# A down projection turned from 96 weight units into 24 rounds of seven products, in a one-core encoder block

## The chip, the cores and the metric
One core of a Trainium2 chip runs the whole block as one program. The metric is the device time of an execution in microseconds.

## The reference, cut to what matters
The block is one layer on x of 512 tokens x 2048 channels, float32: a mixer (attention and a gated recurrence), then a convolutional gated MLP.

```python
h = rmsnorm(x, norm_ffn_pre)
g = causal_dwconv(h @ w_gate, conv_ffn_w, conv_ffn_b)      # w_gate, w_up: 2048 x 6144
y = (gelu(g) * (h @ w_up)) @ w_down                        # w_down: 6144 x 2048
x = x + rmsnorm(y, norm_ffn_post)
```
The change is in the last two lines. The mixer ahead of them keeps its work.

## The kernel before, in words
Every float32 operand of a large product is split into a high part (a ScalarE copy into the matmul's reduced float32 form) and a low part (VectorE: operand minus high part). A product of two 128x128 by 128x256 tiles is three matmuls: high by high, high by low, low by high (`product`, L1816 to L1818). Weights come in units of 128 x 1024 numbers, 512 KB, each partition's 4 KB contiguous in memory. SyncE's queue (SP) issues the weight loads, GpSimd's queue (POOL) issues adding DMAs and stores and reloads of intermediates. Each engine follows its own program in written order and waits on semaphores; `split_done` counts finished low halves of weights and `unit_used` units that TensorE has finished.

**Gate and up projections.** The 48 hidden tiles (128 channels each) are computed 6 plainly and 42 in the seven-product loop (`for i in range(NS)`, NS = 42). A round multiplies a 2 x 2 arrangement of weight blocks by a 2 x 2 arrangement of activation blocks with seven block products instead of eight. Each of the seven is 8 tile products of three matmuls. The rows of the weight arrangement are the gate (A11, A12) and the up (A21, A22) columns of a tile, the four weight sums are S1 = A21 + A22, S2 = S1 + A11, S3 = A21 + A11 and S4 = S2 + A12 (signs are in the operands). S1 and S3 come by a plain load of one block (SP) and an adding DMA of the other onto it (POOL, `add_to_s1`, `add_to_s3`); S2 and S4 are VectorE additions (`form_s2`, `form_s4`). raw_s1 has two buffers, all the others one. SP issues per round i, in this order: S1 (after A22 of the round before), A11 (after the low half of product 0 of round i-1), S3 (after that of product 3), A12 (product 4), A22 (product 6). The high half of product k waits until TensorE has finished product k-3, since the split weights have three places (`w_slot`). The product's regions of the accumulators are taken out by VectorE (and one by ScalarE), become the gate tile, and with convolution and GELU the hidden tile, which POOL stores (`store_h`).

**Down projection.** Four groups of 512 output channels, each 24 units of 256 hidden channels. In a unit, two hidden tiles (reloaded by `load_h`) are the stationary side, as 128 hidden x 128 tokens, and the unit's weights move: 4 banks x 2 halves x 2 tiles x 3 matmuls. y stands with tokens in the partitions. **End.** Sums of squares per token along the row, root and reciprocal, scaling, transposes of y to channels in partitions (`lift`), and VectorE's addition onto x1 (L1807), from where SP stores it.

Of the kernel before, what the change touches and what calls it, by code (L numbers as in the profile page):

```python
# [29 lines left out]
P = 128  # L30
# [31 lines left out]
N_OUT, N_FF, N_FAST, N_HID = U_OUT - U_MIX, U_FF - U_MIX, U_FAST - U_MIX, U_HID - U_MIX  # L62
MORE_MIX = (32, 32)
# [33 lines left out]
H_STEP = 2 * S + 6 * LINE // 4  # L97
# [36 lines left out]
def block_kernel(nc, xT, par_d, weights, gate_w, out):  # L134
    negc_d = nc.dram_tensor("negc", [2 * NP, S], F32, kind="Internal").ap()
    h_d = nc.dram_tensor("h_spill", [FT, P, S], F32, kind="Internal").ap()

    with ExitStack() as ctx:
# [6 lines left out]
        def sem(name):  # L145
# [7 lines left out]
        eps_y = sb("eps_y", [QT])  # L153
# [11 lines left out]

        level = w_all[:, LINE // 4:4 * UW + LINE // 4].rearrange("p (b x) -> p b x", b=2)
        wd_hi, wd_lo = [[level[:, :, S * c:S * c + S] for c in (2 + part, part)] for part in range(2)]
# [5 lines left out]
        DOWN_BANKS = (banks[0:4], banks[4:8])  # L173

        region_a = ExitStack()
        act_hi = sb_in(region_a, "act_hi", [KT, S], F32R)
        act_lo = sb_in(region_a, "act_lo", [KT, S], F32R)
        region_a.close()  # L180
        sb("act_hi_first", [KT // 2, S])
        y_a = sb("y_a", [2, D])
        sb("act_lo_first", [KT // 2, S])
        y_b = sb("y_b", [2, D])
# [61 lines left out]

        ffn = ExitStack()
# [4 lines left out]
        sb_in(ffn, "rest_of_x1_6_7", [UW - HS])  # L252
# [11 lines left out]
        hid = ExitStack()  # L264
        h_t = sb_in(hid, "h_t", [FT, S])
        sb_in(hid, "last_hidden_tile", [5, S])
        y_sq = sb_in(hid, "y_sq", [GROUPS, QT])
        y_p = sb_in(hid, "y_p", [2, QT])
        y_r = sb_in(hid, "y_r", [QT])
        y_s = sb_in(hid, "y_s", [QT])  # L270
        hid.close()
        fin = ExitStack()
        x1_b = sb_in(fin, "x1_b", [KT, S])
        fin.close()

# [3 lines left out]
            wf_landed wf_hi_done wf_split f_done f_low_done f_taken f_ready f_lifted f_negabs f_exp f_logs f_back negc_ready negc_stored negc_spread negc_copied  # L279
# [15 lines left out]
         wf_landed, wf_hi_done, wf_split, f_done, f_low_done, f_taken, f_ready, f_lifted, f_negabs, f_exp, f_logs,  # L295
         f_back, negc_ready, negc_stored, negc_spread, negc_copied,
# [7 lines left out]
         gate_taken, tap_done, conv_done, gelu_done, h_done, h_hi_done, h_split, x1_gained, t_formed,  # L304
         t_hi_done, t_split,
         a11_landed, a12_landed, a22_landed, s3_half, s3_landed, s2_done, s4_done,
         p1_copied, pu_done, pw_done, c22_done, c11_taken, c12_done, c21_done, last_done,
         wd_taken, wdsq_done, y_summed, y_std_done, y_r_done, y_scaled_a, y_scaled_d, diag_done, spread_done,
         eps_y_done, x1_back_landed, lifted, taken,
# [6 lines left out]
        h_stored = [sem(f"h_stored{s}") for s in range(2)]  # L316
        h_landed = [sem(f"h_landed{s}") for s in range(PER_GROUP // 2)]
        s1_half = [sem(f"s1_half{s}") for s in range(2)]
        s1_landed = [sem(f"s1_landed{s}") for s in range(2)]

# [9 lines left out]
        def two_tiles(t, ku):  # L330
            return t[:, bass.ds(ku * 2, 2), :].rearrange("p a s -> p (a s)")

# [9 lines left out]
        def y_tile(i):  # L342
            return y_a[:, i] if i < 2 else y_b[:, i - 2]

        def h_half(t, s):

            c = 4 * S * s + HS - 7 * LINE // 4
            t = flat(t)[:, c:c + 2 * H_STEP].rearrange("p (b x) -> p b x", b=2)[:, :, 0:2 * S]  # L350
            return t.rearrange("p b (a n) -> p b a n", n=S)[:, :, :, 0:HS]

        def h_tokens(t, s, kt, i):

            c = 4 * S * s + HS - 7 * LINE // 4 + H_STEP * kt + S * (i // 2) + P * (i % 2)
            return flat(t)[:, c:c + P]

        def halves(t):
            return t.rearrange("p (b a n) -> p b a n", b=2, n=HS)

# [13 lines left out]
        w3_hi, w3_lo = k_tiles(w_3[:, 0]), k_tiles(w_3[:, 1])  # L374

# [7 lines left out]
        def _(sp):  # L383
# [69 lines left out]
            for i in range(NS):  # L453

                u, q = U_FF + 4 * (PLAIN + i), N_FAST + 7 * (i - 1)
# [8 lines left out]
                sp.dma_start(raw[:, 0], weights[u]).then_inc(a11_landed, 16)  # L464
# [4 lines left out]
                sp.dma_start(raw_s3[:], weights[u + 2]).then_inc(s3_half, 16)  # L469
                sp.wait_ge(split_done, q + 5 if i else N_FAST)  # L470
                sp.dma_start(raw[:, 1], weights[u + 1]).then_inc(a12_landed, 16)
# [4 lines left out]
                sp.dma_start(raw_a22[:], weights[u + 3]).then_inc(a22_landed, 16)  # L476
            sp.wait_ge(split_done, N_HID - 6)
            sp.dma_start(raw[:, 0], weights[U_DOWN]).then_inc(raw_landed[0], 16)
            sp.wait_ge(split_done, N_HID - 2)
            sp.dma_start(raw[:, 1], weights[U_DOWN + 1]).then_inc(raw_landed[1], 16)  # L480
            with sp.Fori(1, GROUPS * PER_GROUP // 2) as t:
                for s in range(2):

                    sp.wait_ge(split_done, t * 2 + (N_HID + s - 1))
                    sp.dma_start(raw[:, s], weights[bass.ds(t * 2 + (U_DOWN + s), 1)].rearrange(
                        "a p n -> p (a n)")).then_inc(raw_landed[s], 16)

            for k in range(KT):
                sp.wait_ge(taken, k + 1)
                sp.dma_start(out[:, k], x1_b[:, k]).then_inc(stored, 16)  # L490
# [4 lines left out]
        def _(pool):  # L495
# [26 lines left out]
            with pool.Fori(1, NP) as p:  # L522
                pool.wait_ge(gw_split, p)
                pool.dma_start(gw[:], gate_w[bass.ds(p, 1)].rearrange("a p m n -> p (a m) n")).then_inc(gw_landed, 16)
                pool.wait_ge(s_taken, p * 6)
                pool.dma_start(negc[:], negc_d[bass.ds(p * 2, 2)].partition_broadcast(P)).then_inc(negc_landed, 16)
# [7 lines left out]
            def store_h(j):  # L534
                pool.wait_ge(h_done, j + 1)
                pool.dma_start(h_d[j], h_out[:, j % 2]).then_inc(h_stored[j % 2], 16)

            def add_to_s1(i):
                pool.wait_ge(s1_half[i % 2], i // 2 * 16 + 16)
                pool.dma_start(raw_s1[:, i % 2], weights[U_FF + 4 * (PLAIN + i) + 3], accum_op=ALU.add).then_inc(  # L540
                    s1_landed[i % 2], 16)

            def add_to_s3(i):
                pool.wait_ge(s3_half, 16 * i + 16)
                pool.dma_start(raw_s3[:], weights[U_FF + 4 * (PLAIN + i)], accum_op=ALU.add).then_inc(s3_landed, 16)

            for j in range(PLAIN - 2):
                store_h(j)
            add_to_s1(0)
            add_to_s3(0)  # L550
            store_h(PLAIN - 2)
            add_to_s1(1)
            for i in range(NS):
                store_h(PLAIN - 1 + i)
                if i + 1 < NS:
                    add_to_s3(i + 1)
                if i + 2 < NS:
                    add_to_s1(i + 2)

            def load_h(n):  # L560
                for e in range(2):
                    pool.wait_ge(h_stored[e], 16 * n + 16)
                half = PER_GROUP // 2
                at_least(pool, h_hi_done, n - half + 1)
                pool.dma_start(h_t[:, 2 * n:2 * n + 2], h_d[2 * n:2 * n + 2].rearrange("a p s -> p a s")).then_inc(
                    h_landed[n % half], 16)

            pool.wait_ge(unit_used, N_HID - 3)
            for n in range(4):
                load_h(n)  # L570
            for n in range(4, PER_GROUP):
                pool.wait_ge(unit_used, N_HID + n - 4)
                load_h(n)
                if n == 8:
                    store_h(FT - 1)

            pool.wait_ge(x1_stored, 16 * KT)
            for q in range(4):
# [1784 lines left out]
```

## Time and profile before

| | |
|---|---|
| median of 3 runs | 2187.09 us (2187.03 to 2187.22) |
| span of the profiled execution | 2186.0 us |
| TensorE / VectorE / ScalarE / GpSimd busy | 2171.7 / 1529.4 / 1002.2 / 141.7 us |
| gate/up loop | from 828 to 1638 us |
| down projection | from 1638 to 2168 us |

The span is the profiled execution's own time; the median of the runs stands 1.1 us above it. Busy matmul time overlaps itself, since matmuls are pipelined (a matmul is shown with 276 ns, and the next starts 0.113 us after it), so the distance between matmuls is read from counts in a window, and not from their mean duration.

### The profile page before, as it was taken

To read this page: it belongs to the slowest core of one execution; us is meant where nothing else is said; L and a number is where in the kernel's file an instruction comes from. 1 tells how busy PE (TensorE), PEld (TensorE's weight loads), DVE (VectorE), ACT (ScalarE), POOL (GpSimd) and SP (SyncE) were. 2 spreads that over 40 slices of the span, in tenths; PEclk is the share of its full clock that TensorE was granted. 3 is DMA by queue.
4 is the path that set the end of the run, shared out by engine and by line. 5 is a ranking of instruction groups with operands and counts; after the bars stand their busy time and mean duration, and the time that the engine had idled before them with its cause. 6 is when DMAs were issued, how large, how long until landed. Compare 5 with 4: busy or idle time off the path is not lost.

```text
span 2186.0 us, 45684 instructions
## 1 busy us (share of the span) xinstructions
PE 2171.7 (99%) x18942; PEld 2154.4 (99%) x18942; DVE 1529.4 (70%) x2030; ACT 1002.2 (46%) x1278; POOL 141.7 (6%) x210
## 2 busy tenths in 40 slices
PE   9999999999999999999999999999999999999998
PEld 8999999999999999999999999999999999999998
DVE  7776777778755977888888888888885444444445
ACT  6555555447322554444444444444443343343433
POOL 0000000000100001111111111111111100000000
PEclk9999999999999999999999999999999999999999
DMA  5222222222432437777777777777767632222343
GB/s 175 91 99 94 85 92 95 89 96 87 150 112 97 163 116 203 209 214 210 209 203 206 209 206 207 209 214 204 204 178 219 192 113 97 96 96 96 99 170 116
DMA packets 100850, 329.01 MB, mean 151 GB/s; under 512 B 13024, under 2 KB 20832, under 8 KB 100208
## 3 DMA queue, kind: packets, MB, share of 16 engines
q1 hardware_dynamic: 75456, 240.06, 31.9%
q0 software_dynamic: 22672, 82.36, 17.5%
q10 hardware_dynamic: 2592, 4.72, 0.6%
q8 instruction: 98, 1.61, 0.3%
q14 instruction: 32, 0.26, 0.0%
HBM read 306.09 MB, written 21.00 MB: 150 GB/s over the span
## 4 chain that ended last, share of the span: by engine, by line
PE 97%; DVE 2%; ACT 1%; issue 0%; POOL 0%; DVEq 0%; ACTq 0%; POOLq 0%
PE bank L1816 31%; PE bank L1818 31%; PE bank L1817 31%; PE bank L1901 1%; PE bank L1914 1%; PE bank L1926 0%; DVE x_b L1807 0%; PE bank L1925 0%; PE bank L1986 0%; ACT w_all L589 0%; DVE w_all L1058 0%; PE bank L1872 0%; PE bank L2004 0%; PE bank L2003 0%; PE bank L1932 0%
## 5 line engine op out<-in xcount | busy, mean ns | idle before, releaser
L1816 PE MATMUL bank<-act_hi,w_all 128*128 128x256 f32 x2832 | 786.3, 278 | 1.7 <-DVE act_lo L1530 0.9
L1818 PE MATMUL bank<-act_hi,w_all 128*128 128x256 f32 x2832 | 782.2, 276 | 0.0
L1817 PE MATMUL bank<-act_lo,w_all 128*128 128x256 f32 x2832 | 782.1, 276 | 0.0
L1816 PEld LDWEIGHTS bank<-act_hi,w_all 128*128 128x128 f32 x2832 | 531.6, 188 | 5.4 <-issue 2.5
L1817 PEld LDWEIGHTS bank<-act_lo,w_all 128*128 128x128 f32 x2832 | 531.7, 188 | 0.4
L1818 PEld LDWEIGHTS bank<-act_hi,w_all 128*128 128x128 f32 x2832 | 531.6, 188 | 0.0
L1816 PE MATMUL bank<-w_all,act_hi 128*128 128x256 f32 x1536 | 424.0, 276 | 0.1
L1818 PE MATMUL bank<-w_all,act_lo 128*128 128x256 f32 x1536 | 423.9, 276 | 0.0
L1817 PE MATMUL bank<-w_all,act_hi 128*128 128x256 f32 x1536 | 423.9, 276 | 0.0
L1068 DVE TENSOR_TENSOR w_all<-raw,w_all 128x1024 fp32r<-128x1024 f32 x95 | 116.4, 1226 | 279.5 <-ACT w_all L595 279.5
L1816 PEld LDWEIGHTS bank<-w_all,act_hi 128*128 128x128 f32 x1536 | 288.3, 188 | 0.3 <-issue 0.3
L1817 PEld LDWEIGHTS bank<-w_all,act_hi 128*128 128x128 f32 x1536 | 288.3, 188 | 0.0
L1818 PEld LDWEIGHTS bank<-w_all,act_lo 128*128 128x128 f32 x1536 | 288.3, 188 | 0.0
L1058 DVE TENSOR_TENSOR w_all<-raw,w_all 128x1024 fp32r<-128x1024 f32 x134 | 164.1, 1224 | 135.8 <-ACT w_all L589 133.9
L1816 PE MATMUL bank<-tsum,w_all 128*128 128x256 f32 x896 | 247.3, 276 | 0.0
L1817 PE MATMUL bank<-tsum,w_all 128*128 128x256 f32 x896 | 247.3, 276 | 0.0
L1818 PE MATMUL bank<-tsum,w_all 128*128 128x256 f32 x896 | 247.3, 276 | 0.0
L595 ACT ACTIVATE w_all<-raw 128x1024 fp32r<-128x1024 f32 x95 | 100.9, 1062 | 288.3 <-PE bank L1818 283.4
L589 ACT ACTIVATE w_all<-raw 128x1024 fp32r<-128x1024 f32 x133 | 140.5, 1057 | 168.0 <-PE bank L1818 165.8
L963 ACT ACTIVATE w_all<-raw_s 128x1024 fp32r<-128x1024 f32 x112 | 119.0, 1062 | 154.0 <-PE bank L1818 149.6
L1677 DVE TENSOR_TENSOR w_all<-raw_s,w_all 128x1024 fp32r<-128x1024 f32 x112 | 137.2, 1225 | 44.8 <-ACT w_all L963 43.4
L1816 PEld LDWEIGHTS bank<-tsum,w_all 128*128 128x128 f32 x896 | 168.2, 188 | 0.0
(297 smaller groups left out, 3707.0 us busy)
## 6 DMA issues: line engine op xcount, KB each, us to landing
raw<-weights SPq DMA_DIRECT2D x310, 512.0 KB, 3.3
raw_s<-weights SPq DMA_DIRECT2D x84, 512.0 KB, 5.0
raw_s<-weights POOLq DMA_DIRECT2D x84, 512.0 KB, 5.7
raw_a<-weights SPq DMA_DIRECT2D x42, 512.0 KB, 5.5
h_spill<-h_out POOLq DMA_DIRECT2D x48, 256.0 KB, 3.4
h_t<-h_spill POOLq DMA_DIRECT2D x24, 512.0 KB, 4.1
x<-xT POOLq DMA_DIRECT2D x16, 256.0 KB, 3.9
out<-x ACTq DMA_DIRECT2D x16, 256.0 KB, 2.3
```

Source lines behind the costliest of these rows:

```text
L589: act.activation(w_hi[s], k_tiles(raw[:, s]), ACT.Copy).then_inc(hi_done, 1)
L595: act.activation(wd_hi[s], out_cols(raw[:, s]), ACT.Copy).then_inc(hi_done, 1)
L963: act.activation(w_slot(q)[0], k_tiles(RAW_OF[n](i)), ACT.Copy).then_inc(hi_done, 1)
L1058: dve.tensor_tensor(w_lo[s], k_tiles(raw[:, s]), word(w_hi[s]), ALU.subtract).then_inc(split_done, 1)
L1068: dve.tensor_tensor(wd_lo[s], out_cols(raw[:, s]), word(wd_hi[s]), ALU.subtract).then_inc(split_done, 1)
L1677: dve.tensor_tensor(lo, k_tiles(RAW_OF[n](i)), word(hi), ALU.subtract).then_inc(split_done, 1)
L1816: pe.matmul(dst, ah, bh, start=start, stop=False, skip_group_check=goes_on)
L1817: pe.matmul(dst, ah, bl, start=False, stop=False, skip_group_check=goes_on)
L1818: return pe.matmul(dst, al, bh, start=False, stop=stop, skip_group_check=goes_on)
L1901: last[e] = pe.matmul(dst, q, k, start=t == 0, stop=t == 2)
L1914: last = pe.transpose(dst, sm[:, c:c + P], ident[:])
```

## The change
The down projection goes through the same loop: NF = NS + 24 rounds. A round computes two tiles of 128 output channels over a chunk of 16 hidden tiles (8 pairs); three chunks (CH = 3) x eight pairs of output tiles (PAIRS_OUT = 8). The seven moving operands of a chunk (quadrants and sums of the hidden tiles) are formed when the hidden tiles are: per pair of tiles VectorE makes the differences in place (`t_of_pair`, `t3_of_pair`), and POOL stores seven parts of 128 KB (`store_pair`, `store_t3`). For each chunk POOL loads them back, 1 MB each (`load_t`), into the places of the operands that the chunk before no longer needs; ScalarE and VectorE split them in place (`t_n_hi`, `t_n_lo`), between the weight halves, as `T_AFTER` says. The weights keep their layout in memory, so a block of 128 x 1024 for a pair of output tiles is now 1024 pieces of 128 numbers (512 B), for plain and for adding DMAs. y has channels in partitions now; its partial sums of the first two chunks go to memory (the second by an adding store), come back as `Y_TILES` and are completed in the third chunk. The ending has no transposes: squares are summed by matmuls, the reciprocal roots are spread over the partitions by two matmuls, 16 tiles are scaled by VectorE, and the additions onto x1 are 4 on VectorE and 12 on GpSimd. A few semaphores of the mixer are merged, and one POOL loop there is written out.

```diff
+CH = 3
+CK = UK
+PAIRS_OUT = KT // 2
+ND = CH * PAIRS_OUT
+NF = NS + ND
+T_AFTER = {1: 5, 2: 6, 3: 7, 4: 8, 5: 9, 6: 10}
...
+        OPERANDS = ((P00, T0, T1, T2, P10, P11, T3), (P01, P00, T0, T1, T2, P10, P11), (T3, P01, P00, T0, T1, T2, P10),
+                    (P11, T3, P01, P00, T0, T1, P10))
+        def t_free_after(c, n):
+            last = N_FAST + 7 * (NS - 1 + PAIRS_OUT * c)
+            if n == 0:
+                return last - 7 if c else N_FAST
+            return last + 7 if c == CH - 1 and n == 6 else last + n
+        def down_weights(i, r, kh):
+            c, o = (i - NS) // PAIRS_OUT, (i - NS) % PAIRS_OUT
+            u, n = U_DOWN + o // 2 * PER_GROUP + CK * c, o % 2 * 2 * P + r * P
+            return weights[u:u + CK].rearrange("u p (t n) -> t p u n", t=2)[kh][:, :, n:n + P]
...
 SP:
-            for i in range(NS):
+            for i in range(NF):
-                sp.dma_start(raw_s1[:, i % 2], weights[u + 2]).then_inc(s1_half[i % 2], 16)
+                if i < NS:
+                    sp.dma_start(raw_s1[:, i % 2], weights[u + 2]).then_inc(s1_half[i % 2], 16)
+                else:
+                    sp.dma_start(in_k(raw_s1[:, i % 2]), down_weights(i, 1, 0)).then_inc(s1_half[i % 2], 16)
...
 POOL:
+            def load_t(c, n):
+                pool.wait_ge(unit_used, t_free_after(c, n))
+                m = CK * (c + 1)
+                for stored_t, each in ((to_stored, 16), (te_stored, 16), (tq_stored, 32), (t3_stored, 16)):
+                    pool.wait_ge(stored_t, each * m)
+                pool.dma_start(operand(NS + PAIRS_OUT * c, n)[3], t_d[c, T_PLACE[n]].rearrange("p (k n) -> p k n", n=HS)).then_inc(t_landed[n], 16)
...
+            for i in range(NF):
+                if i <= NS:
+                    store_after(PLAIN - 1 + i)
+                elif i == NS + 1:
+                    store_t3(HT - 1)
+                c, o = (i + 1 - NS) // PAIRS_OUT, (i + 1 - NS) % PAIRS_OUT
+                if i >= NS - 2 and c + 1 < CH and o == PAIRS_OUT - 1:
+                    load_t(c + 1, 0)
+                if i > NS and i - 1 < NS + 2 * PAIRS_OUT:
+                    store_y(i - 1)
+                at_boundary = i >= NS - 1 and c < CH and o == 0
+                if at_boundary:
+                    load_t(c, 1)
+                if i + 1 < NF:
                     add_to_s3(i + 1)
+                if i + 2 < NF:
                     add_to_s1(i + 2)
+                if at_boundary:
+                    for n in range(2, 6):
+                        load_t(c, n)
+                    if c == CH - 1:
+                        load_y(0)
+                        load_y(1)
+                    load_t(c, 6)
+                if i == NS + 2 * PAIRS_OUT:
+                    for t in range(2, KT):
+                        load_y(t)
...
 ACT (and DVE alike, with the low halves):
+            def t_n_hi(c, n):
+                act.wait_ge(t_landed[n], 16 * c + 16)
+                hi, _, _, summed = operand(NS + PAIRS_OUT * c, n)
+                act.activation(hi, summed, ACT.Copy).then_inc(th_done, 1)
+            def t_n_after(i, n, convert):
+                k = 7 * (i - (NS - 1)) + n
+                for c in range(CH):
+                    if k == 7 * PAIRS_OUT * c - 2:
+                        convert(c, 0)
+                    for m in range(1, 7):
+                        if k == 7 * PAIRS_OUT * c + T_AFTER[m]:
+                            convert(c, m)
+            def hi(i, n):
+                if i < NF:
+                    product_hi(i, n)
+                    t_n_after(i, n, t_n_hi)
...
 DVE, the first region of b in the third chunk, and the end:
+                dve.wait_ge(y_back[o if o < 2 else 0], 32 if o < 2 else 32 + 16 * (KT - 4))
+                chain(dve.tensor_tensor(ya[:, HS:], ya[:, HS:], p1[:], ALU.add))
+                chain(dve.tensor_tensor(in_two(yb), in_two(yb), p1[:].unsqueeze(1).broadcast_to([P, 2, HS]), ALU.subtract))
+                dve.wait_ge(unit_used, N_FAST + 7 * i + 2)
+                dve.tensor_tensor(ya[:, HS:], ya[:, HS:], b, ALU.add).then_inc(pu_done, 1)
+            for t in range(KT):
+                y = Y_TILES[t]
+                dve.scalar_tensor_tensor(out=y, in0=y, scalar=col("g_ffn_post", t), in1=banks[1][:], op0=ALU.mult,
+                                         op1=ALU.mult).then_inc(z_done, 1)
+                if t in ADD_BY_DVE:
+                    dve.wait_ge(z_done, t + 1)
+                    dve.tensor_tensor(x1_place(t), x1_place(t), in_two(y), ALU.add).then_inc(taken_d, 1)
...
 TensorE:
-            for i in range(NS):
+            for i in range(NF):
+                if i >= NS:
+                    pe.wait_ge(tn_split, (i - NS) // PAIRS_OUT * 7 + n + 1)
...
-            for g in range(GROUPS):
-                n, out_banks = g * PER_GROUP, DOWN_BANKS[g % 2]
...
```

## Rows read from the trace of the kernel before

**Rows 1.** The page: span, busy time, and the chain that ended last.
```profile
span 2186.0 us, 45684 instructions
PE 2171.7 (99%) x18942; PEld 2154.4 (99%) x18942; DVE 1529.4 (70%) x2030; ACT 1002.2 (46%) x1278; POOL 141.7 (6%) x210
PE 97%; DVE 2%; ACT 1%; issue 0%; POOL 0%; DVEq 0%; ACTq 0%; POOLq 0%
```
**Rows 2.** Windows: us, busy (count) of PE, PEld, DVE, ACT, POOL, clock, DMA, GB/s.
```profile
1000.00:1200.00 200.00, 200.00 (x1767) 200.00 (x1767) 164.76 (x200) 93.77 (x107) 25.22 (x33) 1.00 0.75 206
...
1900.00:2100.00 200.00, 200.00 (x1767) 200.00 (x1766) 90.94 (x82) 80.17 (x90) 1.65 (x3) 1.00 0.33 111
```
**Rows 3.** Groups by line, down projection: first of its three matmul lines.
```profile
L1816 PE MATMUL bank<-w_all,act_hi 128*128 128x256 f32 x1536 | 424.0, 276 | 0.1
```
**Rows 4.** Timelines of TensorE, VectorE, ScalarE in one round: start, us, instruction, idle before.
```profile
998.35 0.28 PE L1816 MATMUL bank<-act_hi,w_all 128*128 128x256 f32 x1
...
1010.58 1.23 DVE L1677 TENSOR_TENSOR w_all<-raw_a,w_all 128x1024 fp32r<-128x1024 f32 x1 [0.27 <-ACT w_all L963]
...
1013.62 1.22 DVE L1677 TENSOR_TENSOR w<-raw,w 128x1024 fp32r<-128x1024 f32 x1
...
1020.37 1.06 ACT L963 ACTIVATE w<-raw_s 128x1024 fp32r<-128x1024 f32 x1 [0.95 <-PE bank L1818]
```
**Rows 5.** Groups by line and shape, VectorE and ScalarE, 840 to 1640 us.
```profile
L1687 DVE TENSOR_TENSOR raw_s<-raw_s,raw 128x1024 f32<-128x1024 f32 x42 | 51.1, 1217 | 4.0 <-DMA raw_s<-weights 4.0
...
L1734 DVE TENSOR_TENSOR up<-pv,bank 128x256 f32<-128x256 f32 x42 | 17.7, 421 | 1.4
...
L963 ACT ACTIVATE w_all<-raw_s 128x1024 fp32r<-128x1024 f32 x112 | 119.0, 1062 | 154.0 <-PE bank L1818 149.6 <-DVE raw_s L1687 4.4
```
**Rows 6.** Timeline of SP's queue: two loads of 1024 pieces, then one round.
```profile
16.02 3.15 SPq L417 DMA_DIRECT2D ev<-weights  x2
...
1003.67 0.33 SPq L469 DMA_DIRECT2D raw_s<-weights  x1
...
1011.83 0.33 SPq L476 DMA_DIRECT2D raw_a<-weights  x1
1012.20 0.50 SPq L460 DMA_DIRECT2D raw_s<-weights  x1
```
**Rows 7.** Timeline of POOL in the same round; group of the hidden tiles' reload.
```profile
1007.58 0.58 POOL L536 DMA_DIRECT2D h_spill<-h_out  x1 [7.08 <-DVE h_out L1704]
1008.14 0.91 POOL L545 DMA_DIRECT2D raw_s<-weights  x1
1018.95 0.86 POOL L540 DMA_DIRECT2D raw_s<-weights  x1 [9.90 <-DMA raw_s<-weights]
...
L565 POOL DMA_DIRECT2D h_t<-h_spill x24 | 17.1, 712 | 96.5 <-PE bank L1818 91.0 <-issue 5.4
```
**Rows 8.** DMA in windows 5.5 to 7, 10 to 15, 1000 to 1100 us.
```profile
q1 hardware_dynamic: 465, 0.24, 63.0%
...
DMA packets 985, 1.94 MB, mean 388 GB/s; under 512 B 77, under 2 KB 656, under 8 KB 985
...
q0 software_dynamic: 1980, 7.08, 37.8%
q1 hardware_dynamic: 3609, 13.14, 37.1%
```
**Rows 9.** DMA issues: transfer, count, size, median us to landing.
```profile
raw_s<-weights POOLq DMA_DIRECT2D x84, 512.0 KB, 5.7
...
x_b<-out POOLq DMA_DIRECT2D x4, 1024.0 KB, 5.7
```
**Rows 10.** The window after TensorE's last work.
```profile
2181.00:2184.00 3.00, 0.00 (x0) 0.00 (x0) 0.86 (x2) 0.00 (x0) 0.00 (x0) 0.50 1.03 381
```
**Rows 11.** Timelines of ScalarE and VectorE at the end.
```profile
2168.49 0.60 ACT L1004 ACTIVATE sq<-bank 128x512 f32<-128x512 f32 x1
...
2171.24 10.62 DVE L1807 SCALAR_TENSOR_TENSOR x_b<-bank,par,x_b 128x512 f32<-128x512 f32 x16
```

More of the change, by code:

```diff
@@ L245, in block_kernel @@
         spare.close()
+        plain = ExitStack()
+        tsum_f32 = sb_in(plain, "tsum_f32", [4, 2, UK, HS])
+        plain.close()
         ffn = ExitStack()
@@ new lines, in store_y @@
+            def store_y(i):
+                n = i - NS
+                for done in (c11_taken, c12_done, c22_done, c21_done):
+                    pool.wait_ge(done, i + 1)
+                if n == PAIRS_OUT:
+                    for e in range(2):
+                        pool.wait_ge(y_stored[e], 16 * PAIRS_OUT)
+                for half in range(2):
+                    t = n % PAIRS_OUT * 2 + half
+                    if n < PAIRS_OUT:
+                        pool.dma_start(y_d[t], Y_STAGE[n % 2][half]).then_inc(y_stored[n % 2], 16)
+                    else:
+                        pool.dma_start(y_d[t], Y_STAGE[n % 2][half], accum_op=ALU.add).then_inc(y_stored[n % 2], 16)
@@ L583, in _ @@
+                if i == NS + 2 * PAIRS_OUT:
+                    for t in range(2, KT):
+                        load_y(t)
+            adds = [t for t in range(KT) if t not in ADD_BY_DVE]
+            pool.wait_ge(x1_back, 16 * KT)
+            for t in adds:
+                pool.wait_ge(z_done, t + 1)
+                pool.tensor_tensor(x1_place(t), x1_place(t), in_two(Y_TILES[t]), ALU.add).then_inc(taken_p, 1)
         @block.scalar
@@ new lines, in _ @@
+                hi(i + 1, 0)
+                hi(i + 1, 1)
+            act.activation(cols[:, 0, 0:1], eps[:, 0:1], ACT.Sqrt)
+            ya, yb = Y_TILES[KT - 2], Y_TILES[KT - 1]
+            act.wait_ge(yacc_added, KT - 2)
+            for done, src, dst in ((c22_done, yb[:, HS:], pu[:]), (c11_taken, ya[:, 0:HS], sq[:, 1, 0:HS]),
+                                   (c12_done, ya[:, HS:], sq[:, 1, HS:S]), (c21_done, yb[:, 0:HS], pv[:])):
+                act.wait_ge(done, NF)
+                act.activation(dst, src, ACT.Square).then_inc(ysq2_done, 1)
@@ L1805, in _ @@
-            for k in range(KT):
-                dve.wait_ge(lifted, k + 1)
-                dve.scalar_tensor_tensor(out=x1_b[:, k], in0=banks[k % 8][:], scalar=col("g_ffn_post", k),
-                                         in1=x1_b[:, k], op0=ALU.mult, op1=ALU.add).then_inc(taken, 1)
+                if i <= NS:
+                    t_after(j - 1)
+                if square >= 0:
+                    add_y_square(square + 1)
+                lo(i, 5)
+                stage_free(i)
+                c22_of(i)
@@ L1872, in channel_sum @@
                     last = pe.matmul(bank[:], ones[:], src, start=(i == 0), stop=(i == len(srcs) - 1))
-                last.then_inc(sum_done, 1)
-            def column_sum(bank, src):
-                for j in range(QT):
-                    last = pe.matmul(bank[:, j:j + 1], src[:, P * j:P * j + P], ones[:, 0:1], start=True, stop=True)
                 last.then_inc(sum_done, 1)
@@ L2298, in _, with column_sums @@
-            for k in range(4, KT):
-                at_least(pe, taken, k - 7)
-                for i in range(QT):
-                    last = lift(k, i)
-                last.then_inc(lifted, 1)
+                fast_product(i, 5, c, False)
+                fast_product(i, 6, b, False)
+            def column_sums(src, j0, j1, stop):
+                for j in range(j0, j1):
+                    last = pe.matmul(banks[0][:, j:j + 1], src[:, P * (j - j0):P * (j - j0) + P], ones[:, 0:1],
+                                     start=src is acc and j == 0, stop=stop, skip_group_check=True)
+                return last
@@ new lines, in _ @@
+            pe.wait_ge(yacc_added, KT - 2)
+            column_sums(acc, 0, QT, False)
+            pe.wait_ge(ysq2_done, KT - 2 + 3)
+            column_sums(pu, QT // 2, QT, False)
+            column_sums(sq[:, 1], 0, QT, False)
+            pe.wait_ge(ysq2_done, KT - 2 + 4)
+            column_sums(pv, 0, QT // 2, True).then_inc(sum_done, 1)
+            for n in range(2):
+                c = slice(HS * n, HS * n + HS)
+                pe.wait_ge(diag_done, 3 + n)
+                pe.matmul(banks[1][:, c], ones[:], raw_s24[:, c], start=True, stop=True).then_inc(spread_done, 1)
```

716 lines of the change are left out of this document (342 added, 374 removed).

## The prediction, made before the changed kernel was run
> **What bounds the kernel now.** I read the shares first, then the chain, then the windows. TensorE is busy 99% of the span, and the chain is TensorE for 97% [rows 1]. In the seven-product loop and in the down projection alike the granted clock is full, and the matmuls follow each other at 200/1767 = 0.1132 us [rows 2]: so time is the number of matmuls, as long as the engines that feed it are on time. In the loop they are on time by little: VectorE is busy 165 of 200 us and the DMA engines 75%; in the down projection VectorE has 91 of 200 and DMA 33% [rows 2]. So the change takes matmuls out of the relaxed stage and gives it the tight stage's feeding.
>
> **What is removed.** The down projection is 1536 products of three matmuls, 4608 [rows 3]. After, 24 rounds x 7 x 8 x 3 = 4032. 576 fewer, by 0.1132: **-65.2 us**. That is fixed by the loops; if nothing waits, it comes in full.
>
> **How a round is timed.** A product is 24 matmuls = 2.72 us, a round 19.0. Its first matmul starts at 998.35 [rows 4]; I call that 0. ScalarE's high half of product k is formed when TensorE has finished k-3 (its wait ends on TensorE), VectorE's low half after it. The low half of product 6 is done at 1011.81 = 13.4, that of the next round's product 0 at 1014.84 = 16.5, where TensorE wants it at 19.0 [rows 4]. From low half 6 to that point TensorE bears 19.0-13.4 = **5.6 us**; what takes longer stops it.
>
> **The conversions of the new operands.** Each chunk of eight rounds brings seven operands of 128x2048. ScalarE's 1024-wide copy takes 1.06, VectorE's subtraction 1.22 [rows 4, 5]: twice that is 2.1 and 2.4 us each. They stand inside the in-order streams: operand 0 after product 5 of the round before last, operands 1 and 2 after products 5 and 6 of the last round B before the chunk, 3 to 6 after the first four products of the chunk.
>
> **Operand 2, the main term.** Read POOL's program for round B: load operand 1, add to S3(B+1), add to S1(B+2), and only then load operands 2 to 6. SP issues S1(B+2) behind A22(B+1), which waits for low half 6: in the trace A22 goes at 1011.83 and S1 at 1012.20 [rows 6]. POOL's add follows at 1018.95, 7.1 us after A22, with 4 KB pieces [rows 7]. Meanwhile ScalarE stands at operand 2 before it may form B+1's product 0. So from low half 6:
> - A22 and S1 landed: 7.1 with 4 KB pieces. Now each is 1024 pieces of 512 B. SP spent 3.15/2 = 1.6 us on each load of 1024 pieces, against 0.33 to 0.5 [rows 6]; and 512 B pieces came at 465 in 1.5 us, 3.2 ns each, 3.3 us a load, the DMA engines at 63% [rows 8]. I take 10; ends 7.1 and 12.
> - POOL issues the add: 0.9 for 128 pieces; 256 pieces of the hidden load cost 0.13 more than 128 of the store [rows 7]. For 1024, ends 0.9 and 3.5, I take 2.
> - Operand 2: 1 MB, at least 5.7 us from issue for 1 MB in a quiet stretch [rows 9], but the adding DMA, itself 5.7, stands before it in POOL's queue. I take 7.5; ends 6 and 9.
> - Then ScalarE 2.1, VectorE 2.4, the sum S2 1.2, low half 1.2 [rows 4, 5]: 7.0.
>
> Sum 26.5, less 5.6: **20.9 us of stop at each of three boundaries**; ends 15.4 and 25.9.
>
> **Operands 0 and 1.** They are behind POOL's S1 add of the round before, which goes at 1018.95 = 1.6 into the round now [rows 7], with the slower loads at about 6.3; operand 0 is issued then and lands at 13.5 to 14; ScalarE wants it at 9.2. Copy 2.1, low half 2.4 and C22 0.84 follow, to 19.4, and product 5 waits for C22, due at 13.6: 5.8 of stop. Operand 1, behind the add and two stores of y, is issued at 9 and lands at 15.5; 2.1+2.4+0.84+1.2 later, at 22.1, low half 6 is done, 8.7 late. So chunks 1 and 2: 5.8+8.7 before the main wait. If loads stay at today's rows: 1+3; high 8+11. Chunk 0 is worse, since POOL first waits for the hidden tile (1007.58 = 9.2 [rows 7]) and its stores: operand 0 lands at 18.5, C22 is done at 23.9, 10.3 late, and operand 1 at 17.2, so low half 6 at 23.9, 10.5 late.
>
> **Operands 3 to 6.** After the stop TensorE has no lead, and VectorE must do 4 x 2.4 beside 4/7 of its round. A down round costs it 9 passes of 1.22 and 4 of 0.42 [rows 5], 12.7; so 7.3+9.8 = 17.1 against 10.9 of TensorE: **6.3** each, 9 in chunk 0, where the last gate tile is still to be finished.
>
> Boundaries: (5.8+8.7+20.9+6.3) x 2 + (10.3+10.5+20.9+9) = **134 us**. Low end (1+3+15.4+6.3) x 2 + 42 = 93, high (8+11+25.9+7) x 2 + 62 = 166.
>
> A gap also costs clock: once TensorE has gone idle at the end, the granted clock is 0.50 in 2181 to 2184, its 1.2 GHz level [rows 10]. Product 7 at that level is 2.7 us longer, mostly under VectorE's 4 us steps: take 1 each, **+3**. The Trainium skill (TensorE: Matmul & The Clock Gate, "Why this matters for your kernels") says the same of idle gaps between matmul bursts and would have every product until recovery at half rate; by it the term would be nearer 8.
>
> **Inside a chunk.** S3's buffer is single: low half 3, load, add, high half 3. Now 1003.67 to 1008.14 for the load (4.5), the add 5.7 [rows 7, 9], and high half 3 comes at 1020.37 = 16.7 after the load's issue [rows 4]. With 512 B pieces 7 + 2 + 6.5 = 15.5: under 16.7, no stop, by 1.2. An adding DMA of 512 B pieces is nowhere in the trace. In the loop q0 spends 605 us of engine time (37.8% of 1600) on 7.08 MB; 11 adds of 128 pieces have some 540 of it, the five stores the rest: 385 ns for 4 KB, about twice the 200 of q1 (594 us, 2956 pieces over 2 KB) [rows 8], as if it read both sides. Split eight ways that is 48 ns; if instead the extra 185 were a fixed cost per piece, 210. I take 58, since twice the read fits the rows: 2 x 1024 x 58 + 5 x 1024 x 27 ns is 257 of 304 us of engine time a round, y and operands put it near full. Cost taken 0, ends 0 and 2 us x 18. The Trainium skill (DMA: Bandwidth & Descriptors, "Specifications") puts line rate at 512 B and above. The trace disagrees for the SP queue: 0.24 MB in 1.5 us, 160 GB/s, at 512 B against 388 with larger pieces [rows 8]. By the page the S1 step would stay near 7.1, and the boundaries near their low end.
>
> **The hidden tiles' sums.** In the gate/up loop VectorE gets about four 256-wide operations (0.42) per two rounds, 0.8 us a round beside 3.5 idle [rows 2]; POOL's S3 add goes up to 3 us later and has 6 to spare: 0, ends 0 and 5.
>
> **y partials.** Tiles 2 and 3 are loaded behind the S1 add, land at about 11 of a round whose VectorE wants them at 5.5, then two or three passes before product 3 (due 8.2): **+4.5** once, ends 0 and 8. Stores and accumulating stores are off the path.
>
> **The tail.** Before: main matmuls end at 2168.4, the span at 2186.0: 17.6. After, from the last product: C21 0.8, square 0.4, sums 0.3, root 0.3, reciprocal 0.2, two diagonals 0.9, two spreads 1.2: 4.1. Then 16 scalings in 10.6 and four adds of 0.68 on VectorE, and the 4.1 that lie today between its last operation and the end [rows 11]: 21.5, **+4**. POOL's twelve adds are not in the trace; by 0.55 for a 512-wide memset they hide, at twice 0.68 they end 4 later.
>
> **Sum.** 2186.0 - 65.2 + 134 + 3 + 4.5 + 4 = 2266.3. The three runs' median stands 1.1 above the span: **2267 us**.
>
> **Rivals.**
> - *Light stops.* Everything at 4 KB rows: 93 for the boundaries, no y wait: 2187 - 65 + 93 + 4 = 2219, and somewhat less if operand 2's load meets idle queues: down to 2190. For: the pieces at 1 KB and above run at full rate. Against: 3.2 ns per piece. Chance 0.17 (0.04 of it within 0.2%).
> - *The other side: operands hidden, faster.* If the operands landed in time, each boundary would cost only VectorE's excess, 6.3 + 2: 2187 - 65 + 25 + 5 = 2152. It decides at the moment when POOL issues operand 2: before TensorE's product 3 of round B ends, it is this case. For: 65 us are sure, and operands 1 to 6 are spaced one product apart in their waits on TensorE. Against: POOL's order with S1(B+2) in between. Chance 0.12.
> - *DMA the bound.* If an adding 512 B piece costs over 80 ns, the S3 circle is over 19 us in every down round: at 130 ns, 64 x 130 = 8.3 us in place of 3.7, 20.1 + 2.3 = 22.4, +3.4 x 18 = 61: 2267 + 61 = 2328. Decided by load plus add over 16.7. For: 85% or more DMA demand and no row for such a piece. Chance 0.15.
>
> Forecast 0.56. What a measurement can tell from no change is 0.2%, 4.4 us. Faster 0.12, same 0.04, slower 0.84. Range 2200 to 2340; the forecast's own 2235 to 2300.
>
> **What would show it.** 4032 matmuls at 0.113 in the new rounds; three gaps of TensorE of 15 us or more at the chunk boundaries, each ended by VectorE after a ScalarE wait on the DMA of tsum or act; POOL's operand-2 load after its S1 add; VectorE without idle time in the round after; plain rounds at 19.0. It is wrong if operand 2 lands before TensorE runs dry, or if the plain rounds are longer than 19.5.

## The result, and the profile after

The changed kernel takes 2278.2 us in the median of three executions (2275.3 to 2280.1) against 2187.1: 1.042 of the time before, 95% interval 1.040 to 1.043. A fourth execution took 2740 us at a granted clock of 0.74 and is left out as disturbed (with it the median is 2279.1, the figure that the expectations below start from). The forecast was 2267, in a range of 2200 to 2340.

The page of the changed kernel: span, busy time, slices, clock, DMA, and the chain by engine ([rows 1] before).
```profile
span 2276.4 us, 44326 instructions
PE 2134.1 (94%) x18322; PEld 2112.0 (93%) x18322; DVE 1697.1 (75%) x2310; ACT 1029.1 (45%) x1293; POOL 309.5 (14%) x383
PE   9999999999999999999999999999849959975896
PEclk9999999999999999999999999999979989987997
DMA  5233323323534358888878788888769988998996
PE 79%; DMA 8%; DVE 6%; issue 5%; ACT 2%; POOL 1%; POOLq 0%; SPq 0%; DVEq 0%; ACTq 0%
```
TensorE issues 620 fewer matmuls: 576 of the down projection, 64 transposes at the end against 28 small products there now, and 8 fewer ahead of the loop. And it is busy for 94% of a span that is longer. The gaps stand in three places, where the slices show 8 4, 5 and 7 5 8, and in the end. DMA and POOL are in the chain now.

Windows over the three boundaries, the 60 us behind the third, and 60 us of a plain stretch in chunk 0 ([rows 2] before).
```profile
1600.00:1730.00 130.00, 90.18 (x723) 89.19 (x722) 80.53 (x92) 49.89 (x50) 25.19 (x29) 0.84 0.74 192
1800.00:1900.00 100.00, 70.22 (x559) 69.46 (x558) 58.37 (x56) 38.39 (x37) 19.01 (x20) 0.85 0.85 213
2000.00:2100.00 100.00, 62.34 (x464) 61.05 (x463) 53.01 (x51) 34.74 (x32) 20.74 (x21) 0.80 0.90 211
2100.00:2160.00 60.00, 53.77 (x447) 53.38 (x446) 39.44 (x49) 22.39 (x26) 15.35 (x19) 0.94 0.98 223
...
1740.00:1800.00 60.00, 60.00 (x532) 60.00 (x531) 39.86 (x45) 24.89 (x28) 14.92 (x15) 1.00 1.07 224
```
What a window lost is its length less its matmuls times 0.1132 us (the count is the first one in brackets), so it holds both the time in which TensorE stood and the time by which its matmuls were slower: 130 - 81.8 = 48.2, then 36.7 and 47.5, together **132.4 us** at the boundaries; 9.4 in the fourth window. The plain stretch loses nothing: 532 x 0.1132 = 60.2. With the tail (last product 2249.5 to 2276.4, 26.9 against 17.6: +9.3): -65.2 + 132.4 + 9.4 + 9.3 = +85.9 of the 90.4 between the spans. Of the other 4.5, 1.2 stand in chunk 1 and 2.8 ahead of the loop, which starts at 851.6 us where it was 848.7. There the first hidden tiles are computed plainly, and TensorE issues 38 matmuls fewer than before in the same 130 us; 8 of them are gone from the program, the other 30 are 3.4 us (up to 700 us the changed kernel was 0.5 ahead). Before, then after:
```profile
700.00:830.00 130.00, 128.00 (x1107) 126.04 (x1106) 109.26 (x160) 69.88 (x95) 2.17 (x4) 1.00 0.39 130
700.00:830.00 130.00, 126.83 (x1069) 123.40 (x1068) 109.32 (x163) 68.56 (x94) 5.63 (x9) 0.99 0.41 133
```
In the second row TensorE stands 2.2 us for VectorE's low halves of weights, which it doesn't do before. VectorE forms the differences of the first pairs there and POOL stores them; that this is the cause is likely and not tested.

The first boundary, timelines of TensorE, POOL, SP, ScalarE and VectorE ([rows 4, 6, 7] before).
```profile
1687.77 0.55 PE L2005 MATMUL bank<-act_hi,w 128*128 128x256 f32 x1 [15.46 <-issue]
1688.12 0.42 PE L2006 MATMUL bank<-act_lo,w 128*128 128x256 f32 x1
1688.33 0.41 PE L2007 MATMUL bank<-act_hi,w 128*128 128x256 f32 x1
...
1652.14 0.92 POOL L614 DMA_DIRECT2D act_lo_f<-t_spill  x1
1671.82 1.55 POOL L647 DMA_DIRECT2D raw_s<-weights  x1 [17.14 <-DMA raw_s<-weights]
1672.72 2.31 POOL L614 DMA_DIRECT2D tsum_f<-t_spill  x3
...
1665.86 0.37 SPq L528 DMA_DIRECT2D raw_a<-weights  x1
1666.27 0.58 SPq L500 DMA_DIRECT2D raw_s<-weights  x1
...
1659.68 1.91 ACT L1071 ACTIVATE act_hi<-act_lo_f 128x2048 fp32r<-128x2048 f32 x1 [8.32 <-DMA act_lo_f<-t_spill]
1680.83 1.91 ACT L1071 ACTIVATE tsum<-tsum_f 128x2048 fp32r<-128x2048 f32 x1 [18.30 <-DMA tsum_f<-t_spill]
...
1686.45 1.22 DVE L1794 TENSOR_TENSOR w<-raw,w 128x1024 fp32r<-128x1024 f32 x1
```
Read it in the order of the waits. Low half 6 is done at 1665.86, since A22's load goes then. S1's load follows. POOL, idle for 17 us, adds at 1671.82 and only now issues operands 2 to 4, whose places had been free since TensorE's first products of that round. ScalarE has stood 18.3 us at operand 2. The low half that TensorE wants ends at 1687.67, 21.8 us after low half 6, and TensorE starts at 1687.77 after 15.5 us without work. At the second boundary it is 24.0 from low half 6, at the third 23.1.

TensorE's first matmuls after the stop start 0.21 us apart and not 0.113. The granted clock is 0.50 up to 1692, the 1.2 GHz level. The 72 matmuls of the next three products take 10.5 us for 8.2:
```profile
1687.70:1698.30 10.60, 10.53 (x72) 10.53 (x72) 10.57 (x9) 9.27 (x8) 0.00 (x0) 0.77 0.50 151
```

### The profile page after: what moved, and what is told of

The parts are those of the page before. It is cut to its first block, busy times and chain, and to the rows that moved or that the text cites. A ratio compares the mean times of both kernels' runs of the same rounds, so it can differ in the third digit from the quotient of the medians.

```text
span 2276.4 us, 44326 instructions
## 1 busy us (share of the span) xinstructions
PE 2134.1 (94%) x18322; PEld 2112.0 (93%) x18322; DVE 1697.1 (75%) x2310; ACT 1029.1 (45%) x1293; POOL 309.5 (14%) x383
## 4 chain that ended last, share of the span: by engine, by line
PE 79%; DMA 8%; DVE 6%; issue 5%; ACT 2%; POOL 1%; POOLq 0%; SPq 0%; DVEq 0%; ACTq 0%
PE bank L2005 25%; PE bank L2006 25%; PE bank L2007 25%; DMA raw_s<-weights 4%; DMA act_lo_f<-t_spill 2%; DVE w_all L1794 1%; DMA tsum_f<-t_spill 1%; PE bank L2084 1%; PE bank L2097 1%; DVE tsum L1824 1%; DMA t_spill<-h_out 1%; DVE w_all L1153 1%; DVE act_lo L1824 0%; PE bank L2109 0%; PE bank L2108 0%
## 5 line engine op out<-in xcount | busy, mean ns | idle before, releaser
L2005 PE MATMUL bank<-act_hi,w_all 128*128 128x256 f32 x3312 | 924.0, 279 | 40.1 <-issue 17.0
L2006 PE MATMUL bank<-act_lo,w_all 128*128 128x256 f32 x3312 | 918.0, 277 | 0.0
L2007 PE MATMUL bank<-act_hi,w_all 128*128 128x256 f32 x3312 | 917.8, 277 | 0.0
L2005 PEld LDWEIGHTS bank<-act_hi,w_all 128*128 128x128 f32 x3312 | 625.3, 189 | 46.5 <-issue 21.4
L2007 PEld LDWEIGHTS bank<-act_hi,w_all 128*128 128x128 f32 x3312 | 625.2, 189 | 0.0
L2005 PE MATMUL bank<-tsum,w_all 128*128 128x256 f32 x1312 | 366.3, 279 | 36.0 <-issue 18.6
L2006 PE MATMUL bank<-tsum,w_all 128*128 128x256 f32 x1312 | 365.4, 279 | 0.0
L2007 PE MATMUL bank<-tsum,w_all 128*128 128x256 f32 x1312 | 365.2, 278 | 0.0
L2005 PEld LDWEIGHTS bank<-tsum,w_all 128*128 128x128 f32 x1312 | 249.7, 190 | 37.1 <-issue 19.0
L1153 DVE TENSOR_TENSOR w_all<-raw,w_all 128x1024 fp32r<-128x1024 f32 x134 | 164.0, 1224 | 133.4 <-ACT w_all L704 131.6
L2006 PEld LDWEIGHTS bank<-tsum,w_all 128*128 128x128 f32 x1312 | 249.6, 190 | 0.0
L2007 PEld LDWEIGHTS bank<-tsum,w_all 128*128 128x128 f32 x1312 | 249.6, 190 | 0.0
L704 ACT ACTIVATE w_all<-raw 128x1024 fp32r<-128x1024 f32 x133 | 140.6, 1057 | 163.9 <-PE bank L2007 161.5
L2005 PE MATMUL bank<-act_hi,w 128*128 128x256 f32 x576 | 164.2, 285 | 36.1 <-issue 15.7
L2005 PE MATMUL bank<-tsum,w 128*128 128x256 f32 x672 | 186.6, 278 | 5.0 <-DVE pu L1867 4.3
L2006 PE MATMUL bank<-tsum,w 128*128 128x256 f32 x672 | 186.2, 277 | 0.0
L2007 PE MATMUL bank<-tsum,w 128*128 128x256 f32 x672 | 186.2, 277 | 0.0
L2006 PE MATMUL bank<-act_lo,w 128*128 128x256 f32 x576 | 162.7, 283 | 0.0
L2007 PE MATMUL bank<-act_hi,w 128*128 128x256 f32 x576 | 162.6, 282 | 0.0
```

Source lines behind the costliest of these rows:

```text
L704: act.activation(w_hi[s], k_tiles(raw[:, s]), ACT.Copy).then_inc(hi_done, 1)
L1153: dve.tensor_tensor(w_lo[s], k_tiles(raw[:, s]), word(w_hi[s]), ALU.subtract).then_inc(split_done, 1)
L2005: pe.matmul(dst, ah, bh, start=start, stop=False, skip_group_check=goes_on)
L2006: pe.matmul(dst, ah, bl, start=False, stop=False, skip_group_check=goes_on)
L2007: return pe.matmul(dst, al, bh, start=False, stop=stop, skip_group_check=goes_on)
```

## The experiments

Each run is one variant of the changed kernel. The medians stand beside a kernel before of 2187.0 to 2187.3 us. A variant has the edits that its text names, and keeps those of the variant that it is built on.

**1. Order.** Operands 2 to 6 go before the add to S1 at a boundary.
```diff
                     add_to_s3(i + 1)
-                if i + 2 < NF:
-                    add_to_s1(i + 2)
                 if at_boundary:
                     for n in range(2, 6):
                         load_t(c, n)
...
                     load_t(c, 6)
+                if i + 2 < NF:
+                    add_to_s1(i + 2)
```


> One edit to the changed kernel: at the three boundaries POOL issues the loads of operands 2 to 6 (and y tiles 0 and 1) before the add to S1(B+2), not behind it. Theory A (POOL's order makes the stop): the third wait of each boundary, 17 to 22 us from low half 6 to POOL's load of operand 2 in the changed kernel's trace, goes; operand 2 is issued when TensorE has finished product 1, its landing (11 us) then costs some 5 us instead of 20. 2279 falls by 3 x 15 to about 2230 (2215 to 2245). Theory B (the operands' 7 MB on a full DMA make the stop, whatever the order): under 5 us a boundary, 2265 or more. VectorE's excess (6 us a boundary) and the first two waits stay in both.

Measured: 2241.3 us, 37 less, for a change of order with the same bytes. Theory A, at its lower yield; B, with 2265 or more, is out. POOL at the first boundary of this variant: it issues operands 2 to 4 right behind the S3 add and no longer stands 17 us before them:
```profile
1652.94 1.62 POOL L655 DMA_DIRECT2D raw_s<-weights  x1
1653.85 2.34 POOL L614 DMA_DIRECT2D tsum_f<-t_spill  x3
...
1679.64 1.59 POOL L647 DMA_DIRECT2D raw_s<-weights  x1 [8.83 <-DMA raw_s<-weights]
```

**2. Contiguous weights.** The old order, and the host lays each down block out as one 4 KB piece per partition.
```diff
-            return weights[u:u + CK].rearrange("u p (t n) -> t p u n", t=2)[kh][:, :, n:n + P]
+            return weights[U_DOWN + 4 * (i - NS) + 2 * r + kh]
```


> One edit to the changed kernel: the host lays the down weights out so that each block of 128x1024 is one 4 KB piece per partition instead of eight of 512 B; order and bytes are the same. Theory A: each wait that has an S1 load and add in it gets shorter by 2 to 4 us, two to three of them a boundary: 2279 falls by 15 to 30, to 2250 to 2264. Plain rounds stay at 19.0 since TensorE bounds them. Theory C (512 B pieces are the main cost): more than 60 us, under 2220. DMA share in the plain down rounds falls from 1.0 to about 0.8 in both.

Measured: 2249.8 us, 28 less: the upper end of A, far from C's 60. The plain stretch stays as it was, with the same matmuls and a DMA share of 0.81 instead of 1.07:
```profile
1740.00:1800.00 60.00, 60.00 (x532) 60.00 (x531) 41.08 (x46) 24.99 (x28) 8.65 (x12) 1.00 0.81 225
```

**3. Operands 0 and 1 early, too.** With the order of experiment 1; `load_t(c + 1, 0)` and `load_t(c + 1, 1)` stand before the S1 adds of the two rounds before.
```diff
-                if at_boundary:
-                    load_t(c, 1)
...
+                if i >= NS - 3 and c + 1 < CH and o == PAIRS_OUT - 2:
+                    load_t(c + 1, 0)
+                if i >= NS - 2 and c + 1 < CH and o == PAIRS_OUT - 1:
+                    load_t(c + 1, 1)
                 if i + 2 < NF:
                     add_to_s1(i + 2)
```


> The edit of the order, and operands 0 and 1 issued before the S1 adds of the two rounds before as well. Theory A: operand 0 lands before ScalarE wants it (stop 10 in chunk 0 and about 5 in the others goes to 1), operand 1 is issued when TensorE has finished product 0 and lands 11 us later (was 15 to 18): 25 us less than with the order alone, about 2205 (2190 to 2220). Theory B: no better than 2250.

Measured: 2219.3, 22 less than the order alone, at the edge of A's range; B, 2250 or more, is out here as well. TensorE's stops for operands 0 and 1, 47 us in the variant of experiment 1, are down to 8, but its stops for operand 2, 13 in all there, are 39 here: a part of the wait has moved to the next operand.

**4. The same with contiguous weights** (no other edit).

> All loads early and the contiguous weights. Theory A: what is left at a boundary is VectorE's excess and some landing of operands 1 and 2, 10 us each; plus 9 us of longer tail: 2187 - 65 + 30 + 9 = 2161 (2145 to 2185), faster than the kernel before. If the 512 B pieces matter little once the order is right: within 10 us of the version without them.

Measured: 2201.7, 18 less than experiment 3, so the pieces still matter with the order right (less than 10 was the sign that they don't). The direction is right and the size is not: 2161 was expected, 2145 to 2185. The boundaries lose 21 to 24 us each by the sum above, where 10 were expected. The trace shows what I left out: POOL's loads of operands 2 to 6 still stood behind the add to S3(B+1), 8 to 10 us; and the loads, each 1 MB, have medians of 11.6 and 13.7 us to landing.

**5. Operands 2 to 4 before the S3 add** (on the kernel of experiment 4; they go from their place behind it).
```diff
+                if at_boundary:
+                    for n in range(2, 5):
+                        load_t(c, n)
                 if i + 1 < NF:
                     add_to_s3(i + 1)
```


> The early, contiguous version (2202 us), with operands 2 to 4 issued before the add to S3(B+1) as well, each when TensorE has finished the product that frees its place. In the version before this one POOL stood 8 to 10 us before that add, and operand 2 was issued at 10 to 16 us of the round instead of 5.4. Theory A (order): 5 us less at each boundary, 2187 (2180 to 2195). Theory B (the operands' bytes on a full DMA): no gain, since they land no sooner, and the S3 add gets later: 2200 to 2210.

Measured: 2193.7, 8 less; 5 us a boundary were expected, 15 in all, but the time lies in A's range of 2180 to 2195. Issued earlier, the loads take longer: their medians went from 11.6 and 13.7 to 14.9 and 14.5, and in experiment 6 to 17.2 and 15.8. So a part of what the order gains is lost in landing, as B has it; that it is the loads that slow each other was not tested.

**6. Conversions one product later** (on the kernel of experiment 5).
```diff
-T_AFTER = {1: 5, 2: 6, 3: 7, 4: 8, 5: 9, 6: 10}
+T_AFTER = {1: 6, 2: 7, 3: 8, 4: 9, 5: 10, 6: 11}
```


> The same, and operands 1 to 6 converted one product later (after product m+5 instead of m+4; TensorE wants operand m at product m+7). Every load gets 2.7 us more before ScalarE stands at it. If landing still limits: 3 us less a boundary, 8 in all. If VectorE's excess limits (7 conversions of 2.3 us beside its round): within 3 of the version without it.

Measured: 2181.9, 12 less (8 were expected if landing still limited, under 3 if not): landing had still limited. It is faster than the kernel before by 0.2%: 0.9978, interval 0.9968 to 0.9987.

**7. The last additions shared 6 to 10** (on the kernel of experiment 6).
```diff
-ADD_BY_DVE = (3, 8, 12, 15)
+ADD_BY_DVE = (3, 6, 9, 12, 14, 15)
```


> The same as the one with later conversions, and the last additions onto x1 shared 6 on VectorE and 10 on GpSimd instead of 4 and 12. In the changed kernel's trace GpSimd is the end: 12 x 1.36 us from 2256.7 to 2273, while VectorE is done at 2270.9. Two less on GpSimd: 2.7 us less; two more on VectorE: 1.6 more for it. Expected 2 to 3 us less than without. If VectorE and GpSimd slow each other: no gain.

Measured: 2180.8, with runs from 2179.0 to 2183.5: 1.2 less than without, which these runs don't tell from nothing. 0.9969 of the kernel before, interval 0.9956 to 0.9981.

**8. Each operand's low half with a second pass** (on the kernel of experiment 6).
```diff
-                dve.tensor_tensor(lo, summed, word(hi), ALU.subtract).then_inc(tn_split, 1)
+                chain(dve.tensor_tensor(lo, summed, word(hi), ALU.subtract))
+                dve.tensor_tensor(lo, word(lo), word(lo), ALU.max).then_inc(tn_split, 1)
```


> The one with later conversions, and each low half of an operand followed by a second pass of the same width on VectorE that changes nothing (elementwise maximum of the low half with itself), 2.3 us each, seven a boundary, of which four to six lie where TensorE has no lead. If VectorE's excess at the boundaries is what is left of the stop: 4 to 6 x 2.3 x 3 = 28 to 41 us more. If landing of operands is what is left: under 10 more.

Measured: 2224.4, 42.5 more, above the 28 to 41 expected. 21 passes of 2.3 are 48: nearly all of it shows in the time, some 36 of it as stops of TensorE and 6 as slower matmuls behind them. So at the boundaries VectorE's time stands in TensorE's way, once the loads are in order; under 10 more was the sign of the landing alone. Windows over the first boundary, of experiments 7 and 8 (7 differs from 6 in the tail alone): VectorE, the third pair, is busy 84 and 89 of 100 us, with 758 and 617 matmuls.
```profile
1600.00:1700.00 100.00, 88.64 (x758) 87.72 (x757) 84.12 (x96) 51.60 (x51) 20.96 (x29) 0.98 0.86 263
```
```profile
1600.00:1700.00 100.00, 79.33 (x617) 78.14 (x616) 89.00 (x90) 44.13 (x43) 18.40 (x25) 0.88 0.75 234
```

**9. The best order, and the 512 B pieces again.** Experiment 7 with the weights in their old place.

> The best version so far (2181 us: all operand loads in the order in which their places come free, later conversions, six additions on VectorE), with the down weights in their old place again, so 512 B pieces. Taking the pieces away from the changed kernel gained 29 us, and from the early version 18 us; the rest of what they cost is the S1 load before operands 0 and 1, which is out of the way now. Theory A: 8 to 15 us, 2189 to 2196, no faster than the kernel before. Theory C (the pieces fill the DMA engines, and the operands' 7 MB land later in any order): 18 or more, 2199 and up.

Measured: 2199.3, 18.5 more: over A's 8 to 15, at C's 18. Of the 12.8 between the two profiled executions the third boundary has 8.5; windows there, of experiments 7 and 9:
```profile
1980.00:2080.00 100.00, 86.97 (x715) 86.41 (x715) 76.21 (x85) 44.62 (x46) 18.61 (x28) 0.93 0.91 270
```
```profile
1980.00:2080.00 100.00, 79.62 (x640) 78.89 (x640) 69.17 (x76) 42.95 (x43) 27.11 (x32) 0.90 1.06 251
```
Lost, by the same sum as above: 19.1 and 27.6. It is the boundary at which the operands, the y partials and the weights meet, with a DMA share of 1.06. So without another layout in memory the edits of order found here don't make this loop worth its 65 us: 2199.3 is 1.006 of the kernel before, interval 1.005 to 1.007.

**10. Conversions spread over eight products** (on the kernel of experiment 7).
```diff
-T_AFTER = {1: 6, 2: 7, 3: 8, 4: 9, 5: 10, 6: 11}
+T_AFTER = {1: 5, 2: 7, 3: 8, 4: 10, 5: 11, 6: 12}
```


> The best version so far with contiguous weights, and the six conversions spread over eight products (after k = 5, 7, 8, 10, 11, 12 instead of 6 to 11), each before TensorE wants its operand. VectorE's work from product 5 to 12 is 8 x 1.8 + 6 x 2.3 = 28.2 us against 21.8 + 3 of lead, 3.4 over, where it was 24.6 against 16.3 + 3, 5.3 over. Theory A: 2 us less a boundary, 2175. If a conversion right before its product stops TensorE each time: 2181 or more.

Measured: 2180.7, the same as experiment 7; 2175 was expected. That is what the expectation's other theory has, a conversion right before its product stops TensorE each time; no run tells it from a wrong count of the excess.

## Why the prediction was right

The sum came out 11 us low. The main mechanism, POOL's order at the boundaries, is as described; that the boundaries' total fits, 132 for 134 and 3 of clock, is partly luck, since the stops were taken too long and the slow matmuls behind them too few. The timeline of TensorE divides it. Where a matmul starts over 0.3 us later than 0.113 behind the one before, the table counts a stop; what the others take over 0.113 each, it counts as slow matmuls.

| at the three boundaries, us | forecast | stops | slow matmuls behind them |
|---|---|---|---|
| operands 0 and 1 | 49.8 | 46.4 | 11.3 |
| operand 2 | 62.7 | 50.6 | in the next row |
| operands 3 to 6 | 21.6 | 11.5 | 12.7 |
| clock | 3 | | |
| sum | 137 | 108.5 | 24.0 |

By the windows the three lost 132.4; 1.2 of it is a stop at 2002.95, again for S1's data, ahead of the third boundary. The rows above are read matmul by matmul and come to the same within 2 us.

- **What is removed**, -65.2. TensorE's count and its distance of 0.113 us in the plain rounds are as forecast.
- **Operand 2, the main term.** The wait exists as described, at all three boundaries; experiment 1 shows it is POOL's order. Its size was taken at 26.5 us from low half 6 and is 21.8, 24.0 and 23.1. S1's load was mis-sized: POOL adds 6.0, 7.2 and 6.0 us after A22's issue, where I took 10. POOL's add held its queue for 0.9, not 2, though it has 1024 pieces. The operand took 8.1, 9.4 and 9.7 from issue (taken: 7.5). So the stop is 17.4 in the mean, 52 in all instead of 63.
- **Operands 0 and 1.** Each stops TensorE at product 5, which waits for VectorE's C22 behind the conversion: 10.9 and 9.3 us in chunk 0, 4.8 and 5.8, 11.7 and 4.1 in the others. The loads, taken at 6.5 to 7.5 us, took 6.9 and 7.5 in chunk 0 and 9.2 to 12.1 in the other two. Over all of a kernel's operands the medians are higher; the groups of the changed kernel, by issue ([rows 9] before):
```profile
raw_s<-weights POOLq DMA_DIRECT2D x132, 512.0 KB, 6.5
...
act_lo_f<-t_spill POOLq DMA_DIRECT2D x11, 1024.0 KB, 11.8
tsum_f<-t_spill POOLq DMA_DIRECT2D x10, 1024.0 KB, 11.4
```
  Before, the only 1 MB loads stood in a quiet stretch (5.7 [rows 9]).
- **The clock, the term that was mis-sized most.** It was put at 3 us, one for each boundary's product 7, with 8 as the other value. But TensorE stands four times or more at each boundary, and its matmuls start 0.21 us apart behind every long stop: some 24 us in all. Behind operand 2's stop they lie partly under VectorE's work, as the prediction says, and operands 3 to 6 with the clock come to 24.2 for a forecast of 24.6. Behind operands 0 and 1 they are 11.3 us that no term held. How much would come back at the full clock no run shows; with shorter stops less is lost: in 1600 to 2200 us 15 in experiment 6, against 28 in the changed kernel.
- **Operands 3 to 6.** VectorE's excess was given as 6.3 a boundary, 9 in chunk 0. The stops are half of it, as above. Experiment 8, on a later variant, adds seven passes a boundary and 14 us: each costs nearly its own length. It shows that VectorE's time counts there, and not the size of the excess in the changed kernel.
- **The hidden tiles' sums**, 0 forecast, ends 0 and 5: in the loop it is 0 (6355 matmuls in 840 to 1560 us, 0.1133 each); in the plain part ahead of it, which the term didn't look at, 3.4 are lost.
- **Inside a chunk.** No stop was forecast, and the plain stretch of chunk 0 has none (chunk 2 has one, see the y partials). An adding piece of 512 B was taken at 58 ns; in a stretch of chunk 2 with weights alone q0 spends 276 us of engine time on 4198 of them, 66 ns, and q1 29 ns a piece (27 taken). DMA of 2160 to 2200 us:
```profile
q1 hardware_dynamic: 10400, 5.24, 47.6%
q0 software_dynamic: 4198, 2.12, 43.1%
```
  The Trainium skill puts line rate at 512 B and above (DMA: Bandwidth & Descriptors, "Specifications"). For plain pieces the trace is near it: eight of 512 B take 8 x 29 = 232 ns where one of 4 KB took 200; for adding pieces it is 8 x 66 = 528 against 385. In chunk 1 the circle did run over. The chain there goes by S3 alone, 1927.21 to 1946.88, 19.7 us for a round of 19.0: the accumulating stores of y stand in POOL's queue ahead of S3's add, which takes 12.5 us to land. TensorE lost only 1.2 us in 1900 to 2000, and 0.8 of that not by S3 but at 1963, where VectorE had stood 3.9 for S1's data before it could form S2.
```profile
1927.21 1.07 ACT w_all L1065
1928.31 1.24 DVE w_all L1794
1929.56 4.43 DMA raw_s<-weights
1934.37 12.49 DMA raw_s<-weights
1946.88 1.07 ACT w_all L1065
```
- **y partials**, 4.5 forecast, 9.4 measured: tiles 2 and 3 stop product 3 as described, VectorE stands 3.67 us for them and TensorE 2.5. A stop of 4.1 us at 2136.5 to 2140.6 I had not forecast: ScalarE's half of S3 comes late. S3's load is issued by SP at 2112.01 with POOL's 14 loads of y tiles (2108.3 to 2116, 3.7 MB) around it, and POOL's add waits 14.7 us for it, to 2126.71; ScalarE has its data at 2136.68. Slow matmuls behind this stop are 3 us more. Here the S3 circle did stop TensorE; that the burst beside it made it late is argued from the times.
```profile
2115.65 0.42 DVE L1872 TENSOR_TENSOR tsum_f<-tsum_f,p 128x256 f32<-128x256 f32 x1 [3.67 <-DMA tsum_f<-y_parts]
```
- **The tail**, +4 forecast, +9.3 measured. From the last product to the first scaling it is 6.3 us where 4.1 were added up. VectorE's scalings and additions take 15.1 for 13.3: beside GpSimd's additions one of its own takes 0.8 to 1.5 instead of 0.68, a scaling up to 0.73. GpSimd's additions, the unseen row whose upper bound (twice 0.68) was the right one, end 2.3 us after VectorE: three take 4.17.
```profile
2256.71 4.17 POOL L695 TENSOR_TENSOR act_hi_f<-act_hi_f,tsum_f 128x512 f32<-128x512 f32 x3 [32.28 <-DVE tsum_f L1993]
...
2266.55 1.46 DVE L1997 TENSOR_TENSOR tsum_f<-tsum_f,h_out 128x512 f32<-128x512 f32 x1
```
- **The rivals.** "Operands hidden, faster" failed at the point that was named for it: POOL issued operand 2 at the boundary after TensorE had run dry. It comes true in small with the edits of experiments 1 to 7, 2181 us. "DMA the bound" needed over 80 ns for an adding piece; it is 66. "Light stops" had operand 2's wait at its low end, 15.4 us a boundary; it was 17.4, and operands 0 and 1 and the y partials were not light.

## What to carry to other kernels

Where a queue carries loads for different consumers, write beside each issue what its wait hangs on: here loads whose places were free stood behind an add that a later round needs. The order alone cost 37 us, more than the 28 that the 512 B pieces cost. Price a stop with the slow matmuls behind it: here 109 us of stops brought 24 us of them. Before a busy stage's scheme is moved into a stage with slack, count what the stage boundary adds in the engine that has the least slack (VectorE: seven passes of 2.3 us within two rounds), since there little hides it. An estimate of a transfer from a quiet stretch is a lower bound and not a value: 5.7 there, 6.9 to 12.1 here.

## What the runs showed of the hardware that was not expected

- Adding DMAs of 1024 pieces are issued by POOL in 0.9 us, as those of 128 are: the timeline shows 1.55 to 1.62 for one, but the next issue starts 0.9 later. And SP's 0.37 to 0.58 for most such loads is not the 1.6 of [rows 6]; some of them take 0.9 to 3.6.
- A DMA share of 1.05 to 1.07 in a stretch, with 532 matmuls in 60 us, cost TensorE nothing here.
- Behind each long stop of TensorE the granted clock is at its 1.2 GHz level (0.50), and 13 to 28 matmuls start about 0.21 us apart before the distance is 0.113 again.
